# Hybrid decoder layer on one core: the query projection reads the residual times the norm weight, and the root of its norm is applied to the attention scores

## The chip, the cores and the metric

One core of a Trainium2 chip (trn2) runs the whole program as one launch. TensorE (PE), VectorE (DVE), ScalarE (ACT), GpSimd (POOL) and SyncE (SP) work in parallel and wait for one another by semaphores; SyncE issues nearly all DMA. TensorE's clock has two levels, 1.2 and 2.4 GHz, and the profile shows which one was granted. The metric is the device time of a launch in microseconds, the median of several runs.

## The reference

One step of a decoder layer for 264 tokens of width 2048: one prompt of 256 and 8 sample sequences of one token. All data is fp32. Cut to the part around the change:

```python
mix = concat(s5_out, m2_out) @ w_out            # 2048 x 2048
x = x + mix
xn = rmsnorm(x, norm_xa_w)                      # x / sqrt(mean(x^2) + eps) * w
q = (xn @ xa_wq)                                # 4 heads of 512
s = einsum('blhd,bmhd->bhlm', q, k) * 512 ** -0.5
att = softmax(s)                                # over 256 memory tokens
x = x + einsum('bhlm,bmhd->blhd', att, v) @ xa_wo
x = x + hier_moe(rmsnorm(x, norm_ffn_w))        # 32 experts
```

The prompt's keys and values are computed in the kernel from 256 memory tokens; those of the 8 samples are caches in HBM (keys and values of 8 x 256 x 4 x 512).

## The kernel before

Activations are held transposed: 16 blocks of 128 features (partitions) by 264 tokens, XT for the residual, xn for the input of a projection. A projection with a 2048 x 2048 weight takes 8 slabs of 2 MB (256 output columns each), streamed by SyncE through a ring of four slots. TensorE makes one output block of 128 features out of 16 fp32 matmuls (128x128 weights, 264 columns; the trace counts two passes for each). A slab is two blocks, and its slot is reloaded once its second block is done.

The work is cut into stages, each an `nc.Block`; all engines meet at its end before any begins the next. The stages around the change:

1. **Gate and norms** (lines 1503 to 1545). VectorE's `norm_dve` (367) writes the normed Mamba half into `xn[:, 8:16]` and, last in the stage, the normed S5 half into `xn[:, 0:8]`. Their sources u and z are blocks of `h`, which lies in `H`, a part of the buffer SH.
2. **`project_add_norm("w_out", ...)`** (1554). SyncE first issues two "side slabs" of sample keys (`put_side`, 230) into SH, then w_out's slabs in a loop (`load_matrix_loop`) and, with `load_through`, the first query slabs as slots come free. `project_pe` (292) runs the 16 blocks in a loop on TensorE. Per block VectorE adds the result into XT (1598), ScalarE squares it (355) and GpSimd adds the square into block 0 of sqA (1587). Behind block 15: TensorE sums over partitions by a matmul with ones (1578), ScalarE takes the root (357), VectorE the reciprocal (370), and 16 `scalar_tensor_tensor` (372) write xn = XT * weight * 1/root. The same function, with the experts' norm and the router's weights, runs behind attention for xa_wo.
3. **Attention** (1642 to 2018). TensorE runs the 16 query blocks (1801, unrolled, four per head) in two PSUM banks, ScalarE copies each into Q (1945). In the blocks of head h + 1 TensorE also does the small work of head h: GpSimd widens the sample queries (1685), TensorE turns them into rows (1698), spreads each over the partitions (1710), and VectorE multiplies them by the sample keys in a side slab (1887); prompt scores (1718), row maxima (1866, 1867), exponentials on ScalarE with `scale=SCALE` (1962), transposes of the weights (1728), outputs (1741). Head 3 has no further query block over it. The sample values come through the ring, except those of head 2, which take the two side slabs once head 3's keys are used up (`side_used`, 1892, then 1662 to 1666); `sample_outputs` (1761) waits for them. SyncE's queue then goes on with xa_wo's slabs.

What sets the order in the attention stage is the program order of each engine, written out by hand, with semaphore counts; SyncE's program order (1651 to 1667) mixes query slabs, keys and values.

## Time and profile before

| | |
|---|---|
| Runs | 1696.13 us median of 3 (1691.56 to 1696.76) |
| The profiled execution | 1695.85 us, span of its instructions 1694.1 us |
| Mean granted TensorE clock | 0.958 of full |
| Busy: TensorE matmul, weight load | 1554.9 us (92%), 1095.4 us (65%) |
| Busy: VectorE, ScalarE, GpSimd | 743.7, 323.3, 213.9 us |
| DMA | 376.17 MB, mean 222 GB/s |

How to read it: times are from the start of the span. A row of a timeline gives the start, the duration, the engine, the line of the kernel, the operation with what it writes and reads, how many of them run together, and in brackets how long the engine had been idle and what released it. PEld is TensorE's weight load, which overlaps its matmuls. Ends of matmuls are modelled.

### The profile page before, as it was taken

The numbers are of one execution on the slowest core, as the hardware profiler recorded it, in microseconds if no ns is written. First come the engines' busy times: TensorE is split into PE (matmuls) and PEld (weight loads), VectorE is DVE, ScalarE is ACT, GpSimd is POOL, SyncE is SP. The second block draws the span as 40 slices with busy tenths as digits, with TensorE's granted clock in tenths as the row PEclk, the third lists the DMA queues.
The fourth block names the chain that finished last, engine by engine and source line by source line (L and its number), as shares of the span: only waits on it lengthen the run. The fifth ranks groups of instructions, "written<-read, shape, count | busy, mean of one in ns | idle before, by whom it ended". The sixth has DMA issues, their size and how long they took to land. (4 is left out here: it accounts for less than half of the span.)

```text
span 1694.1 us, 20979 instructions
## 1 busy us (share of the span) xinstructions
PE 1554.9 (92%) x8111; PEld 1095.4 (65%) x8111; DVE 743.7 (44%) x2004; ACT 323.3 (19%) x857; POOL 213.9 (13%) x305
## 2 busy tenths in 40 slices
PE   7999998989889788997999699958999999999996
PEld 5888876767677676886888378735445445445444
DVE  3537429999974642002334300061333333333344
ACT  3111101111022321000111100032212212212214
POOL 1111026565620000110000001120000000000000
PEclk9999998999999899998999899968999999999999
DMA  9743443333341556442576866404999999999981
GB/s 275 229 150 113 137 150 112 112 112 112 112 139 67 172 173 218 146 146 92 176 257 232 300 197 233 160 39 168 400 403 403 383 403 401 385 405 402 382 335 51
DMA packets 203311, 376.17 MB, mean 222 GB/s; under 512 B 24931, under 2 KB 158351, under 8 KB 178370
## 3 DMA queue, kind: packets, MB, share of 16 engines
q1 hardware_dynamic: 198554, 370.62, 60.1%
q10 hardware_dynamic: 4664, 4.28, 0.7%
q8 instruction: 62, 1.02, 0.2%
q14 instruction: 31, 0.25, 0.0%
HBM read 363.44 MB, written 11.54 MB: 221 GB/s over the span
## 5 line engine op out<-in xcount | busy, mean ns | idle before, releaser
L923 PE MATMUL ps<-ring,M 128*128 128x256 f32 x1024 | 247.7, 400 | 1.6 <-ACT M L936 1.6
L306 PE MATMUL ps<-X,ring 128*128 128x264 f32 x1024 | 232.0, 390 | 7.5 <-PEq L1503 6.4
L923 PEld LDWEIGHTS ps<-ring,M 128*128 128x128 f32 x1024 | 201.9, 201 | 43.0 <-issue 14.5
L306 PEld LDWEIGHTS ps<-X,ring 128*128 128x128 f32 x1024 | 197.0, 193 | 42.4 <-issue 8.1
L2393 PE MATMUL ps<-ring,M 128*64 128x512 f32 x1024 | 223.3, 594 | 0.3 <-ACT M L2482 0.3
L636 PE MATMUL ps<-X,ring 128*128 128x264 f32 x896 | 204.6, 389 | 0.0
L636 PEld LDWEIGHTS ps<-X,ring 128*128 128x128 f32 x896 | 170.4, 192 | 29.3 <-issue 0.4
L2393 PEld LDWEIGHTS ps<-ring,M 128*64 128x64 f32 x1024 | 72.2, 137 | 137.7 <-issue 137.0
L1801 PE MATMUL ps<-X,ring 128*128 128x264 f32 x512 | 120.2, 392 | 9.4 <-PEq L1555 9.4
L1801 PEld LDWEIGHTS ps<-X,ring 128*128 128x128 f32 x512 | 98.4, 194 | 27.3 <-issue 9.8
L2437 PE MATMUL ps<-SH,M 128*64 128x512 f32 x512 | 113.4, 595 | 1.4 <-DVE XT L2610 1.4
L1598 DVE TENSOR_TENSOR XT<-XT,ps 128x264 f32 x32 | 13.7, 430 | 220.9 <-PE ps L306 220.9
L2599 DVE TENSOR_TENSOR work<-ps,SH 128x512 f32<-128x512 f32 x64 | 44.3, 692 | 142.4 <-ACT SH L2512 142.4
L2405 PE MATMUL ps<-SH 128*128 128x264 bf16 x512 | 90.3, 280 | 3.8 <-DVE work L2604 3.8
L2610 DVE TENSOR_TENSOR XT<-XT,ps 128x264 f32<-128x264 f32 x256 | 88.8, 426 | 1.7 <-PE ps L2405 1.7
L2592 DVE SCALAR_TENSOR_TENSOR M<-M,work,ps 128x256 f32<-128x256 f32 x16 | 7.7, 481 | 171.4 <-ACT M L2489 171.4
L2437 PEld LDWEIGHTS ps<-SH,M 128*64 128x64 f32 x512 | 36.2, 137 | 67.5 <-issue 67.5
L1587 POOL TENSOR_TENSOR M<-M 128x264 f32<-128x264 f32 x30 | 22.2, 741 | 445.3 <-ACT M L355 445.3
L2376 PE MATMUL ps<-SH,M 128*128 128x224 bf16 x512 | 72.2, 265 | 6.1 <-issue 6.1
L2405 PE MATMUL ps<-SH,work 128*128 128x264 bf16 x256 | 71.5, 279 | 0.0
L355 ACT ACTIVATE M<-XT 128x264 f32<-128x264 f32 x48 | 18.6, 418 | 237.4 <-DVE XT L1598 228.2
L2405 PEld LDWEIGHTS ps<-SH 128*128 128x128 bf16 x512 | 34.6, 98 | 40.8 <-issue 12.2
(444 smaller groups left out, 1789.7 us busy)
## 6 DMA issues: line engine op xcount, KB each, us to landing
SH<-in_moe_w_down SPq DMA_DIRECT2D x32, 2048.0 KB, 12.6
ring<-in_moe_w_gate SPq DMA_DIRECT2D x64, 1024.0 KB, 11.9
ring<-in_moe_w_up SPq DMA_DIRECT2D x64, 1024.0 KB, 14.2
ring<-in_w_in SPq DMA_DIRECT2D x14, 2048.0 KB, 8.8
ring<-in_xa_wk SPq DMA_DIRECT2D x8, 2048.0 KB, 9.2
ring<-in_xa_wv SPq DMA_DIRECT2D x8, 2048.0 KB, 9.1
ring<-in_w_out SPq DMA_DIRECT2D x8, 2048.0 KB, 8.8
SH<-in_cache_mem_k SPq DMA_DIRECT2D x8, 2048.0 KB, 9.8
```

Of the source, the lines that this page charges most:

```text
L306: mm = nc.tensor.matmul(ps[:, b, 0:T], w[:, k, o * P:(o + 1) * P], xn[:, k, :], start=(k == 0), stop=(k == KB - 1))
L355: nc.scalar.activation(sq[:, k, 0:n], src[:, k, 0:n], ACT.Square).then_inc(squares.sem, squares.up())
L636: mm = nc.tensor.matmul(ps[:, n % 4, 0:T], w[:, d, o * P:(o + 1) * P], xn[:, d, :], start=(d == 0), stop=(d == KB - 1))
L923: mm = nc.tensor.matmul(ps[:, kv_bank(s), a * 256:(a + 1) * 256], memT[:, k, a * P:(a + 1) * P], w[:, k, :], start=(k == 0), stop=(k == KB ...
L1587: nc.gpsimd.tensor_tensor(sqA[:, 0, :], sqA[:, 0, :], sqA[:, k, :], ALU.add).then_inc(squares_added.sem, squares_added.up())
L1801: mm = nc.tensor.matmul(ps[:, k % 2, 0:T], w[:, d, o * P:(o + 1) * P], xn[:, d, :], start=(d == 0), stop=(d == KB - 1))
L2376: mm = nc.tensor.matmul(ps[:, 6 + f % 2, (k % 2) * 4 * CAP:(k % 2 + 1) * 4 * CAP], x_parts[part][:, a, k * P:(k + 1) * P], picked[:, q % 2 ...
L2393: mm = nc.tensor.matmul(ps[64 * e:64 * e + 64, 0, :], xg[:, p % 3, k, e, :], gate_up_unit(e, half)[:, :, k % 8, :], start=(k == 0), stop=( ...
L2405: mm = nc.tensor.matmul(ps[:, 2 + d % 4, 0:T], out_parts[i][:, d * P:(d + 1) * P], slot_of[:, p % 2, :], start=(i == 0), stop=(i == 2))
L2437: mm = nc.tensor.matmul(ps[64 * e:64 * e + 64, 2 + n, :], g_midT[:, f * P + 64 * e:f * P + 64 * e + 64], down_unit(e)[:, f, 512 * n:512 * ...
L2599: v.tensor_tensor(out_rest[:, c], ps[:, 2 + n, :], out_parts[0][:, c], ALU.subtract).then_inc(outs_rest.sem, 1)
L2610: v.tensor_tensor(XT[:, d, :], XT[:, d, :], ps[:, 2 + d % 4, 0:T], ALU.add).then_inc(scatter_taken.sem, 1)
```

## The change

- The w_out projection becomes a stage of its own. It reads its input from `h`, so the gate stage writes the normed halves there (z in place, S5 into u) and xn is free.
- Per block of it ScalarE now writes xn = XT * weight, without the root, and then the square; for block 15 the copy alone. GpSimd adds the squares of blocks 0 to 14. The ones matmul, root, reciprocal and 16 scalings are not in this stage.
- In the attention stage ScalarE first squares block 15 (into the buffer `rstd`). Behind query block 0 TensorE does six small matmuls (`sums`): sums of squares of the prompt tokens as two columns (tokens on partitions), and of the 8 samples as 8 columns equal in all partitions. ScalarE takes the root of these 10 columns, VectorE the reciprocal and, for the prompt, the product with 512 ** -0.5.
- The prompt's scale goes into the row maxima and the exponentials; that of the samples into GpSimd's widening, now a multiplication.
- Q moves to the start of H, where `h` is no longer needed. So the second half of the second side slab moves behind it, and that slab is loaded by two DMAs of 1 MB instead of one of 2 MB, each time.

```diff
@@ -227,11 +227,20 @@
+SIDE_LOADS = (16, 32)
+def side_part(i, j, n=1):
+    at = 4096 * i + 512 * j if 8 * i + j < 12 else 6144 + 4224 + 512 * (j - 4)
+    return SH[:, at:at + 512 * n]
...
     i = u % 2
-    sp.dma_start(unit(4 + i).rearrange("p (j d) -> p j d", d=DX), of_samples(name, u)).then_inc(
-        side_loaded[i].sem, side_loaded[i].up(16))
+    n = 8 // (i + 1)
+    for j in range(0, 8, n):
+        sp.dma_start(side_part(i, j, n).rearrange("p (j d) -> p j d", d=DX),
+                     of_samples(name, u)[:, j:j + n, :]).then_inc(side_loaded[i].sem, side_loaded[i].up(16))
@@ -289,7 +298,7 @@
-def project_pe(pe, name, first_slab=0, count=None):
+def project_pe(pe, name, source, first_slab=0, count=None):
@@ -303,7 +312,7 @@
             for k in range(KB):
-                mm = nc.tensor.matmul(ps[:, b, 0:T], w[:, k, o * P:(o + 1) * P], xn[:, k, :],
+                mm = nc.tensor.matmul(ps[:, b, 0:T], w[:, k, o * P:(o + 1) * P], source[:, k, :],
@@ -1537,11 +1546,11 @@
     def _(dve):
-        norm_dve(dve, z, xn[:, 8:16, :], m2_wc, 8, T, 1)
+        norm_dve(dve, z, z, m2_wc, 8, T, 1)
...
             nc.vector.tensor_tensor(xn[:, o, :], sig[:, o, :], u[:, o, :], ALU.mult).then_inc(gated.sem, gated.up())
-        norm_dve(dve, xn, xn, s5_wc, 8, T, 2)
+        norm_dve(dve, xn, u, s5_wc, 8, T, 2)
@@ -1550,15 +1559,52 @@
     "router_coarse_weights_loaded", "router_fine_weights_loaded", "squares_added"))
+last_square = rstd[:, 0:T]
+weighted = signal("weighted_block_ready")
+with nc.Block() as block:
+    @block.sync
+    def _(sp):
+        for u in range(2):
+            put_side(sp, "cache_mem_k", u)
+        load_matrix_loop(sp, "w_out", 40)
+        load_through(sp, 44)
+    @block.tensor
+    def _(pe):
+        project_pe(pe, "w_out", h)
+    @block.scalar
+    def _(act):
+        for k in range(KB):
+            act.wait_ge(block_taken.sem, block_taken.at(k + 9))
+            nc.scalar.activation(xn[:, k, :], XT[:, k, :], ACT.Copy, scale=w_xa[:, k:k + 1]).then_inc(
+                weighted.sem, weighted.up())
+            if k < KB - 1:
+                nc.scalar.activation(sqA[:, k, :], XT[:, k, :], ACT.Square).then_inc(squares.sem, squares.up())
+    @block.gpsimd
+    def _(pool):
+        for k in range(1, KB - 1):
+            pool.wait_ge(squares.sem, squares.at(k + 1))
+            if k > 1:
+                pool.wait_ge(squares_added.sem, squares_added.at(k - 1))
+            nc.gpsimd.tensor_tensor(sqA[:, 0, :], sqA[:, 0, :], sqA[:, k, :], ALU.add).then_inc(
+                squares_added.sem, squares_added.up())
+    @block.vector
+    def _(dve):
+        def take(k, b):
+            x = XT[:, bass.ds(k, 1), :]
+            return nc.vector.tensor_tensor(x, x, ps[:, b:b + 1, 0:T], ALU.add)
+        project_take(dve, "w_out", take)
+Signal.stage()
...
             first, n = G[name]
-            if name == "w_out":
-                for u in range(2):
-                    put_side(sp, "cache_mem_k", u)
@@ -1573,7 +1619,7 @@
         def _(pe):
-            project_pe(pe, name)
+            project_pe(pe, name, xn)
@@ -1601,16 +1647,14 @@
-project_add_norm("w_out", w_xa, 44)
-Q = H[:, 2048:2048 + KB * T].rearrange("p (k t) -> p k t", t=T)
+Q = H[:, 0:KB * T].rearrange("p (k t) -> p k t", t=T)
...
 nmax, rsum = (st8[:, 16 * i:16 * i + 8].rearrange("p (h a) -> p h a", a=2) for i in range(2))
+q_root, q_scale, row_scale = st8[:, 32:42], st8[:, 48:58], st8[:, 64:66]
@@ -1631,6 +1675,7 @@
      "sample_weights_zeroed", "sample_queries_widened"))
+q_sums, q_rooted, q_scaled = (signal(f"att_{n}") for n in ("square_sums_done", "roots_ready", "scales_ready"))
@@ -1682,8 +1727,11 @@
                 pool.wait_ge(qt_done.sem, qt_done.at(h))
-            gp.tensor_copy(q_wide, Q[:, 4 * h:4 * h + 4, TP:T].unsqueeze(2).to_broadcast([P, 4, 16, TS])).then_inc(
-                wide_copied.sem, wide_copied.up())
+            else:
+                pool.wait_ge(q_scaled.sem, q_scaled.at(1))
+            gp.tensor_tensor(q_wide, Q[:, 4 * h:4 * h + 4, TP:T].unsqueeze(2).to_broadcast([P, 4, 16, TS]),
+                             q_scale[:, 2:10].unsqueeze(1).unsqueeze(1).to_broadcast([P, 4, 16, TS]),
+                             ALU.mult).then_inc(wide_copied.sem, wide_copied.up())
@@ -1765,15 +1813,15 @@
                     pe.wait_ge(side_loaded[half].sem, side_loaded[half].n)
-                    v = by_sample(unit(4 + half))
+                    value = lambda j, a: side_part(half, 2 * j + a)
...
                     pe.wait_ge(*loaded(g))
-                    v = by_sample(slot(g))
+                    value = lambda j, a: by_sample(slot(g))[:, j, a, :]
...
                         mm = nc.tensor.matmul(ps[32 * j:32 * j + 32, SPV, :], sPT[:, h, a, 4 * half + j, :],
-                                              v[:, j, a, :], start=(half == 0 and a == 0),
+                                              value(j, a), start=(half == 0 and a == 0),
@@ -1787,6 +1835,18 @@
             mm.then_inc(ft_done.sem, ft_done.up())
+        def sums():
+            pe.wait_ge(squares.sem, squares.at(1))
+            parts = (sqA[:, 0, :], last_square)
+            for a in range(2):
+                for i, x in enumerate(parts):
+                    nc.tensor.matmul(ps[:, 7, a:a + 1], x[:, a * P:(a + 1) * P], ones[:, 0:1],
+                                     start=(i == 0), stop=(i == 1))
+            for i, x in enumerate(parts):
+                mm = nc.tensor.matmul(ps[:, 7, 2:10], ones[:, :], x[:, TP:T], start=(i == 0), stop=(i == 1))
+            mm.then_inc(q_sums.sem, q_sums.up())
@@ -1802,6 +1862,8 @@
                     mm.then_inc((q_done if o == 0 else slab_used).sem, (q_done if o == 0 else slab_used).up())
+                if k == 0 and d == KB - 1:
+                    sums()
@@ -1864,7 +1926,7 @@
             st(v.tensor_reduce(nmax[:, h, :], ps[:, SCORE, :].rearrange("p (a m) -> p a m", a=2), AX.X, ALU.max))
-            v.tensor_scalar(nmax[:, h, :], nmax[:, h, :], -SCALE, None, ALU.mult).then_inc(
+            v.scalar_tensor_tensor(nmax[:, h, :], nmax[:, h, :], -1.0, row_scale, ALU.mult, ALU.mult).then_inc(
@@ -1878,13 +1940,12 @@
                 i = b // 4
-                dve.wait_ge(side_loaded[i].sem, side_loaded[i].at(16 * h))
+                dve.wait_ge(side_loaded[i].sem, side_loaded[i].at(SIDE_LOADS[i] * h))
             dve.wait_ge(qrow_done.sem, qrow_done.at(n + 1))
-            keys = by_sample(unit(4 + b // 4))
...
                     dve.wait_ge(sscore.sem, sscore.at(2 * n + a))
-                v.tensor_tensor_reduce(junk8, keys[:, b % 4, a, :], ps[:, 3 + n % 2, :], 1.0, 0.0,
+                v.tensor_tensor_reduce(junk8, side_part(b // 4, 2 * (b % 4) + a), ps[:, 3 + n % 2, :], 1.0, 0.0,
@@ -1917,6 +1978,10 @@
+        dve.wait_ge(q_rooted.sem, q_rooted.at(1))
+        st(v.reciprocal(q_scale, q_root))
+        v.tensor_scalar(row_scale, q_scale[:, 0:2], SCALE, None, ALU.mult).then_inc(q_scaled.sem, q_scaled.up())
+        dve.wait_ge(q_scaled.sem, q_scaled.at(1))
@@ -1960,7 +2025,7 @@
                 nc.scalar.activation(Pm[:, h % 2, a, :], ps[:, SCORE, a * MEM:(a + 1) * MEM], ACT.Exp,
-                                     bias=nmax[:, h, a:a + 1], scale=SCALE,
+                                     bias=nmax[:, h, a:a + 1], scale=row_scale[:, a:a + 1],
@@ -1990,10 +2055,15 @@
+        nc.scalar.activation(last_square, XT[:, KB - 1, :], ACT.Square).then_inc(squares.sem, squares.up())
...
             take_query(4 * q)
+            if q == 0:
+                act.wait_ge(q_sums.sem, q_sums.at(1))
+                nc.scalar.activation(q_root, ps[:, 7, 0:10], ACT.Sqrt, scale=1.0 / D,
+                                     bias=eps_c[:, 0:1]).then_inc(q_rooted.sem, q_rooted.up())
```

## Rows read from the trace of the kernel before

**Rows 1.** The page: busy time of the engines, and GB/s in 40 equal slices.

```profile
PE 1554.9 (92%) x8111; PEld 1095.4 (65%) x8111; DVE 743.7 (44%) x2004; ACT 323.3 (19%) x857; POOL 213.9 (13%) x305
GB/s 275 229 150 113 137 150 112 112 112 112 112 139 67 172 173 218 146 146 92 176 257 232 300 197 233 160 39 168 400 403 403 383 403 401 385 405 402 382 335 51
```

**Rows 2.** Timeline of the seam between the w_out stage and the attention stage.

```profile
765.75 8.17 PE L306 MATMUL ps<-X,ring 128*128 128x264 f32 x36
766.96 0.43 DVE L1598 TENSOR_TENSOR XT<-XT,ps 128x264 f32 x1 [6.69 <-PE ps L306]
...
774.08 0.43 DVE L1598 TENSOR_TENSOR XT<-XT,ps 128x264 f32 x1 [6.69 <-PE ps L306]
774.54 0.42 ACT L355 ACTIVATE M<-XT 128x264 f32<-128x264 f32 x1 [6.70 <-DVE XT L1598]
...
775.84 0.71 PE L1578 MATMUL ps<-M,ones 128*128 128x264 f32 x2 [1.91 <-POOL M L1587]
...
777.10 1.80 DVE L370 RECIPROCAL rstd<-rstd 128x264 f32<-128x264 f32 x1 [2.59 <-ACT rstd L357]
778.94 6.56 DVE L372 SCALAR_TENSOR_TENSOR X<-XT,par,rstd 128x264 f32<-128x264 f32 x16
...
786.00 11.18 PE L1801 MATMUL ps<-X,ring 128*128 128x264 f32 x37 [9.45 <-PEq L1555]
```

**Rows 3.** Stretches: PE, PEld, DVE, ACT, POOL busy; clock, DMA share, GB/s.

```profile
776.00:778.00 2.00, 0.55 (x2) 0.13 (x2) 0.90 (x1) 0.48 (x1) 0.00 (x0) 0.96 1.05 358
786.00:800.00 14.00, 14.00 (x51) 11.53 (x52) 0.00 (x0) 0.38 (x1) 2.45 (x6) 0.80 0.00 1
```

**Rows 4.** Waits in 780 to 1000: who waited for what, total, times, longest.

```profile
PE ps L1775 <- DMA SH<-in_cache_mem_v: 11.7, 1, 11.7
```

**Rows 5.** Timeline of the seam between the attention stage and the xa_wo stage.

```profile
980.83 0.66 PE L1787 MATMUL ps<-ident,M 128*128 128x128 f32 x4 [0.71 <-ACT M L1991]
981.52 0.26 DVE L1916 COPY X<-ps 128x16 f32<-128x16 f32 x2 [4.68 <-PE ps L1787]
982.59 9.74 PE L306 MATMUL ps<-X,ring 128*128 128x264 f32 x35 [1.10 <-PEq L1642]
```

**Rows 6.** Timeline of attention where head 3's queries are widened.

```profile
924.15 0.61 POOL L1685 COPY SH<-SH 128x512 f32<-128x512 f32 x1 [35.02 <-ACT SH L1945]
925.30 0.91 PE L1698 MATMUL ps<-ident,SH 128*128 128x128 f32 x6 [1.41 <-ACTq L1982]
```

**Rows 7.** Busy time by stretch, around that idle time.

```profile
920.00:930.00 10.00, 8.59 (x45) 7.02 (x43) 2.43 (x6) 2.75 (x6) 0.61 (x1) 1.00 1.05 388
```

**Rows 8.** Busy time by stretch, at the seam before xa_wo.

```profile
980.00:990.00 10.00, 8.19 (x34) 6.54 (x31) 0.26 (x2) 0.59 (x1) 0.00 (x0) 0.83 1.07 348
```

**Rows 9.** Timeline of TensorE at 512, small matmuls among projections.

```profile
512.33 0.29 PE L1223 MATMUL ps<-wtmp,tri 128*128 128x16 f32 x2
...
513.14 1.54 PE L923 MATMUL ps<-ring,M 128*128 128x256 f32 x6
```

**Rows 10.** Timeline of attention where head 0's queries are widened.

```profile
817.91 0.61 POOL L1685 COPY SH<-SH 128x512 f32<-128x512 f32 x1 [28.90 <-ACT SH L1945]
820.82 1.05 PE L1698 MATMUL ps<-ident,SH 128*128 128x128 f32 x8
```

**Rows 11.** GpSimd's groups by line and shape, busy and mean ns.

```profile
L1037 POOL TENSOR_TENSOR X<-X,wtmp 128x256 f32<-128x256 f32 x32 | 30.3, 946 | 2.5
L2130 POOL TENSOR_TENSOR M<-M 128x512 f32<-128x512 f32 x4 | 4.5, 1151 | 12.8 <-ACT M L2166 12.8
```

**Rows 12.** Busy time by stretch, before and in the wait for the last value slab.

```profile
937.00:941.00 4.00, 4.00 (x33) 1.34 (x36) 3.13 (x12) 0.59 (x1) 0.00 (x0) 1.00 0.01 2
943.00:945.00 2.00, 2.00 (x25) 0.66 (x18) 1.70 (x5) 0.00 (x0) 0.00 (x0) 1.00 0.77 256
945.00:967.00 22.00, 8.79 (x60) 5.09 (x52) 4.55 (x18) 2.90 (x6) 0.00 (x0) 0.81 1.05 387
```

**Rows 13.** Busy time by stretch, between attention and the experts.

```profile
1116.00:1150.00 34.00, 19.39 (x107) 12.51 (x106) 16.07 (x51) 11.40 (x23) 10.56 (x14) 0.70 0.01 2
```

## The prediction

> **What bounds the kernel now.** I read from coarse to fine: the page's busy shares, busy time by stretch, the timeline of each seam between stages, the granted clock there, then the waits. The page gives TensorE 92% of the span [rows 1]: what lets TensorE start earlier shortens the kernel unless a later wait takes it back. In the stretch of the change a projection block of 16 matmuls takes 7.12 us, the distance between two of VectorE's additions into XT (766.96 to 774.08), and the blocks follow each other without a gap [rows 2].
>
> The hole is at the seam. The last w_out block is added at 774.08 and its square taken at 774.54; GpSimd adds that, TensorE sums over partitions at 775.84, and behind the root come VectorE's reciprocal at 777.10 (1.80 us) and the 16 scalings of the norm, 6.56 us from 778.94. TensorE starts the query projection at 786.00. Between the end of its last w_out matmul (765.75 + 8.17 = 773.92) and 786.00 it did 0.71 us of work [rows 2]. The hole also costs clock: the granted clock is full (2.4 GHz) up to just before 778, and of the 14 us from 786 to 800 its mean of 0.80 means 5.6 us at half (1.2 GHz) [rows 3].
>
> A second hole lies in the same stage: TensorE waits 11.7 us, once, for a value slab by DMA in the third head's sample outputs [rows 4]. The page's chain of waits is of no use here, since it holds only the last 25 us.
>
> **Part 1, the norm leaves the seam.** Removed between the last addition and the query projection: the last square with its addition, the sum matmul, the root, the reciprocal, 16 scalings. Left: the addition (774.08, 0.43 us) and one ScalarE instruction, the copy times weight of block 15. Its nearest row is the square of the same shape, 0.42 us from 774.54, so it ends at 774.96 [rows 2]. Then the barrier between stages. At the other seam where TensorE comes without long idle time, VectorE's last copies end at 981.52 + 0.26 = 981.78 and TensorE starts at 982.59: 0.81 us [rows 5]. At the present one it is 786.00 - (778.94 + 6.56) = 0.50 us, after a long wait [rows 2]. I take 0.81, because TensorE now also has to leave its loop just then: start at 775.77, **10.2 us earlier**. Ends: 775.46 with 0.50 us; and 776.65 if leaving the loop is what ends last, since TensorE's first instruction behind the loop stands at 775.84 and 0.81 follows. So 9.4 to 10.5 us. SyncE's issue of the last query slab waits for the same matmul as VectorE's addition and is shorter than what follows that: it doesn't hold the barrier.
>
> **Part 2, the clock.** The gap becomes 773.92 to 775.77, 1.85 us, with full work on both sides. A TensorE idle time of 1.41 us inside the query stage (before 925.30, [rows 6]) left the clock at 1.00 for the whole stretch 920 to 930 [rows 7]. I take it that it holds: 5.6 us at half speed were 2.8 us lost, and **2.8 us** come back. Against it speaks the seam at 980 to 983: idle times of 0.71 and 1.10 us with four transposes between them [rows 5], and a clock of 0.83 over 980 to 990, so 3.4 us at half and 1.7 us lost [rows 8]. The Trainium skill ("TensorE: Matmul & The Clock Gate", its parts on the clock gate and on transposes) says that idleness throttles the array and that transposes do not count as busy in the same way. By that the seam at 980 was emptier than its busy time says, and a poor model of a gap between plain matmuls; this trace cannot separate the two.
>
> **Part 3, what is put in.** (a) Six fp32 matmuls of 1 or 8 columns behind query block 0, on TensorE's path. Nearest: four fp32 matmuls of 16 columns with 128x128 weights between projections, 512.33 to 513.14 (the first of the four and what follows them), 0.20 us each [rows 9]; six make **1.2 us**. Fewer columns might make them cheaper, so the low end is half, 0.6; the high end is the form with 128 columns, 1.05 us for four [rows 10], 1.6 us for six. Their wait for the last square (ScalarE, at the start of the stage) is over long before block 0 ends. (b) The root of 10 columns on ScalarE, reciprocal and scale on VectorE: covered by query block 1 (7.12 us), since VectorE has nothing before the first head's rows, ScalarE's next job is taking block 1, and GpSimd's first widening comes after block 3. Without that cover, at most the 1.80 us of the 264-column reciprocal and a ScalarE instruction of 0.42. (c) Per block of w_out a second ScalarE instruction, 0.42 us in a period of 7.12 us: nothing. (d) Scales given as columns in the exponentials and the row maxima change no counts: nothing. (e) GpSimd's widening of the sample queries becomes a multiplication of two inputs on 128x512. Now it takes 0.61 us; a two-input operation of that size took 1.15 us (L2130) [rows 11]. Before heads 0 to 2 there is room: it starts at 817.91 and TensorE uses it at 820.82, 2.9 us [rows 10]. For head 3 TensorE comes at once: 924.15 + 1.15 = 925.30, just when TensorE now starts, since it is also held by ScalarE's exponential [rows 6]; with the weight load in front I take **0.1 us**. Ends: 0; and 0.8 us at GpSimd's dearest rate, 946 ns for 256 elements (L1037) [rows 11], which makes 1.89 us for 512.
>
> The Trainium skill ("ScalarE: Activation LUTs", what a table load costs) charges 2.66 us for a switch of function set. The root moves from one stage to the next; should that bring one more switch, uncovered, the sum would be smaller by that figure.
>
> **Part 4, the side slabs.** One more issue at the start of the w_out stage, whose first slabs are loaded by then, and four later on SyncE; key slabs are fetched a head ahead. The last value slab is the exposed one. It lies behind three other slabs in the queue: together 8.4 MB, of which 0.5 move from 943 to 945 at 256 GB/s and the other 7.9 need 20.4 us at 387 GB/s, to 965.4; TensorE goes on at 967, since the next weights mix in [rows 12]. Two halves move the same bytes in the same place: **0**. Ends: 1.9 us gained if the mixing goes; half a slab more of other traffic in front of the second half, 1.0 MB at 387 GB/s, 2.7 us lost.
>
> **Does the gain pass on?** The 11.7 us wait ends with a burst of value slabs, and the burst starts when VectorE has scored half of head 3: from 937 to 941 DMA moved 2 GB/s [rows 12]. So it moves with the stage and the wait keeps its length. Behind attention DMA is idle from 1116 to 1150 (2 GB/s) [rows 13], so the expert stage, in which the queues run full at 380 to 405 GB/s [rows 1], starts when compute lets it.
>
> **Sum.** 10.2 + 2.8 - 1.2 - 0.1 = 11.7 us. The profiled execution took 1695.85 us (span 1694.1), so 1684.15; the median of the runs, 1696.13, lies 0.3 above it: **1684.4 us**, 0.7% less.
>
> **Rivals.**
> - *The clock falls all the same* (15%), as at 982: 1.7 us lost again, 1684.4 + 1.7 = 1686.1 us. For it: the look of that seam. Against: 1.41 us of idle time without a fall. The skill's rule on transposes makes it the less likely.
> - *A DMA wait takes the gain back* (10%). If the burst of value slabs does not move with the stage, the 11.7 us wait grows by the whole gain: 1696 us. For it: it is TensorE's largest wait for DMA in this stretch. Against: the idle queue just before.
> - *GpSimd's multiplication is slow in this form* (5%), the one on the slower side. Its scale is read with a step of zero in two dimensions, which no GpSimd row shows. A duration p costs 3(p - 2.9) + (p - 1.1) us over the four heads. That cancels the 11.8 us of the rest at p = 5.4 us and makes the kernel 5 us slower at p = 6.7 us: 1701 us. Against: no row with 256 columns is above 0.95 us.
> - *The forecast's mechanism*: 70%.
>
> **From these to the numbers.** 0.3%, about 5 us, is what a measurement of this kernel can tell from no change. Forecast and first rival are faster by more than that: 0.85. The second is the same: 0.10. The third is slower: 0.05. Within the forecast the best ends give 10.5 + 2.8 - 0.6 + 1.9 = 14.6 us (1681.5), the worst 9.4 + 2.8 - 1.6 - 0.8 - 2.7 = 7.1 us (1689.0). With a microsecond on either side for the median's own scatter: 1680.5 to 1690.0, which takes in the first rival and leaves out the other two, 15%.
>
> **What the profile of the changed kernel would show.** Right: TensorE idle less than 2.5 us between w_out and the query projection, the clock at 1.00 there, 16 scalings and a 1.80 us reciprocal gone from VectorE, query block 1 later by 1.2 us, GpSimd's widening at about 1.15 us. Wrong: half clock in the first query block; a wait for the last value slab well off 11.7 us; idle time at the query transposes of heads 0 to 2; a table load more on ScalarE's path.

## The result and the profile after

The changed kernel takes **1678.92 us** (median of 4 runs, 1676.59 to 1680.68), the kernel before on the same chip 1693.85 us (4 runs, 1691.08 to 1696.76): ratio 0.9905 [0.9884, 0.9926], 14.9 us less. The forecast was 1684.4 us, 11.7 us less, range 1680.5 to 1690.0: the time lies below the range. What the forecast worked out at the seam came nearly to the number; the rest of the gain came from places to which it gave nothing.

The page of the changed kernel, busy time by engine, against [rows 1]:

```profile
span 1678.9 us, 21005 instructions
PE 1550.0 (92%) x8121; PEld 1093.6 (65%) x8121; DVE 735.7 (44%) x1989; ACT 330.2 (20%) x873; POOL 215.4 (13%) x304
```

TensorE is busy for 4.9 us less though it has 10 more instructions: some matmuls ran at full clock that ran at half before. The span is 15.2 us shorter. So most of the gain, 10.3 us, is idle time. The timeline of the seam between w_out and attention, against [rows 2]:

```profile
774.60 0.43 DVE L1599 TENSOR_TENSOR XT<-XT,ps 128x264 f32 x1 [6.69 <-PE ps L315]
775.06 0.51 ACT L1581 ACTIVATE X<-XT,par 128x264 f32<-128x264 f32 x1 [6.29 <-DVE XT L1599]
...
775.86 0.42 ACT L2058 ACTIVATE rstd<-XT 128x264 f32<-128x264 f32 x1 [0.28 <-PEq L1565]
...
776.03 7.36 PE L1861 MATMUL ps<-X,ring 128*128 128x264 f32 x32 [1.59 <-PEq L1565]
...
783.22 0.28 PE L1845 MATMUL ps<-ones,M 128*128 128x1 f32 x2
...
783.42 0.38 ACT L2010 COPY SH<-ps 128x264 f32<-128x264 f32 x1 [7.14 <-PE ps L1861]
...
784.48 15.82 PE L1861 MATMUL ps<-X,ring 128*128 128x264 f32 x70
...
784.66 0.27 ACT L2065 ACTIVATE M<-ps,eps_c 128x10 f32<-128x10 f32 x1 [0.86 <-PE ps L1848]
...
784.96 0.22 DVE L1982 RECIPROCAL M<-M 128x10 f32<-128x10 f32 x1 [9.94 <-ACT M L2065]
...
791.88 0.38 ACT L2010 COPY SH<-ps 128x264 f32<-128x264 f32 x1 [6.95 <-PE ps L1861]
```

From the last addition to TensorE's first query matmul it takes 776.03 - 774.60 = 1.43 us; it was 11.92 us. The sums, the root and the reciprocal lie behind block 0, and no wait arises from them. Stretches of the changed kernel (columns as in rows 3), against [rows 3]:

```profile
774.00:776.00 2.00, 0.44 (x2) 0.03 (x2) 0.43 (x1) 0.66 (x2) 0.16 (x1) 1.00 0.24 54
...
786.00:800.00 14.00, 14.00 (x65) 11.97 (x64) 0.00 (x0) 0.76 (x2) 0.00 (x0) 1.00 0.47 151
```

The clock stays at 1.00 across a stretch of 2 us in which TensorE is busy for 0.44, and then there are 65 matmuls in 14 us where 51 were.

**Where the 15.2 us come from.** I read the distance between pairs of events that both kernels have (us, the profiled execution of each). "Query block taken" is ScalarE's copy of that block; an addition is VectorE's into XT:

```
stretch                                           before  after   diff  forecast
last w_out addition - query block 1 taken          22.02   8.82 -13.20  -13.0
query block 1 - block 2 taken (the sums)            7.12   8.46  +1.34   +1.2
block 2 - block 16 taken                          120.49 120.49   0.00    0
block 16 taken - first late value slab issued      18.04  17.80  -0.24   +0.1
that issue - TensorE on behind the last slab       25.57  25.48  -0.09    0
there - first xa_wo addition ("xa_wo seam")        24.49  21.94  -2.55    0
xa_wo additions 1 to 16                           106.80 106.80   0.00    0
16th addition - second expert down-projection
  slab issued ("norm and router")                  88.74  87.00  -1.74    0
there - first store of y                          499.07 499.13  +0.06    0
sum                                               912.34 895.92 -16.42  -11.7
```

Ahead of this stretch and behind it the changed kernel lost 0.5 and 0.7 us; that was not followed up. The part ahead differs between traces by more than that: the last w_out addition stands at 771.4 to 776.1 us in the 17 traces of this document, so the distances compare kernels better than whole spans do. Every row that the forecast worked out is right to 0.4 us. The surplus sits in two rows, far behind the change, to which it gave nothing: 4.3 us.

Timeline and stretches of the changed kernel around these two places; against [rows 5, 8] for the first:

```profile
968.43 0.66 PE L1835 MATMUL ps<-ident,M 128*128 128x128 f32 x4 [0.70 <-ACT M L2056]
...
970.04 9.16 PE L315 MATMUL ps<-X,ring 128*128 128x264 f32 x40 [0.96 <-PEq L1687]
...
977.59 0.43 DVE L1644 TENSOR_TENSOR XT<-XT,ps 128x264 f32 x1 [8.21 <-PE ps L315]
```

```profile
943.00:961.00 18.00, 8.40 (x40) 2.60 (x33) 0.10 (x2) 0.58 (x1) 0.00 (x0) 0.64 1.07 371
967.00:977.00 10.00, 8.34 (x43) 6.41 (x36) 0.26 (x2) 0.58 (x1) 0.00 (x0) 1.00 1.06 333
1084.00:1104.00 20.00, 8.82 (x41) 5.86 (x40) 14.14 (x35) 6.58 (x11) 1.51 (x4) 0.74 0.27 105
1111.00:1137.00 26.00, 12.96 (x70) 9.38 (x71) 12.91 (x43) 7.57 (x17) 8.21 (x12) 0.54 0.01 3
```

The same four of the kernel before, as far as they do not stand ahead, 13 to 17 us later:

```profile
991.81 0.43 DVE L1598 TENSOR_TENSOR XT<-XT,ps 128x264 f32 x1 [10.04 <-PE ps L306]
```

```profile
956.00:974.00 18.00, 6.68 (x27) 3.26 (x28) 0.00 (x0) 0.94 (x2) 0.00 (x0) 0.62 1.07 368
1098.00:1118.00 20.00, 8.82 (x36) 5.57 (x35) 14.15 (x35) 6.58 (x11) 1.51 (x4) 0.66 0.28 105
1128.00:1154.00 26.00, 14.56 (x81) 10.77 (x82) 11.32 (x41) 6.27 (x15) 6.54 (x11) 0.54 0.01 2
```

At the xa_wo seam the instructions are the same and the gaps nearly so, 0.70 and 0.96 us beside 0.71 and 1.10; but the clock does not fall. The granted clock read microsecond by microsecond gives the stretches at half clock (TensorE's busy time in them in brackets). Before: 777-792, which is 13.7 us (5.5); 958-973, 13.7 (5.0); 982-986, 3.4 (3.4); 1102-1116, 13.7 (5.5); 1129-1154, 23.9 (13.9). After: none at the first seam; 942-946, 3.4, and 949-960, 10.2 (3.6 behind the wait); none at the xa_wo seam; 1089-1100, 10.2 (3.1); 1112-1137, 23.9 (12.7). Half of the busy time at half clock is lost. At the xa_wo seam that is (3.4 + 5.0 - 3.6) / 2 = 2.4 us of the 2.55; in norm and router (5.5 + 13.9 - 3.1 - 12.7) / 2 = 1.8 of 1.74. So both extra gains are clock: the same work lost less to half clock. Why the clock steps elsewhere in the same work is what the experiments are about.

### The profile page after: what moved, and what is told of

It reads as the page before. It is cut to its first block and busy times, and to the rows that moved or that the text cites. A ratio compares the mean times of both kernels' runs of the same rounds, so it can differ in the third digit from the quotient of the medians.

```text
span 1678.9 us, 21005 instructions
## 1 busy us (share of the span) xinstructions
PE 1550.0 (92%) x8121; PEld 1093.6 (65%) x8121; DVE 735.7 (44%) x1989; ACT 330.2 (20%) x873; POOL 215.4 (13%) x304
## 5 line engine op out<-in xcount | busy, mean ns | idle before, releaser
L645 PE MATMUL ps<-X,ring 128*128 128x264 f32 x896 | 205.1, 390 | 0.0
L645 PEld LDWEIGHTS ps<-X,ring 128*128 128x128 f32 x896 | 171.0, 192 | 29.2 <-issue 0.4
L315 PE MATMUL ps<-SH,ring 128*128 128x264 f32 x512 | 116.1, 391 | 6.4 <-PEq L1512 6.4
L1861 PE MATMUL ps<-X,ring 128*128 128x264 f32 x512 | 117.7, 387 | 1.6 <-PEq L1565 1.6
L315 PE MATMUL ps<-X,ring 128*128 128x264 f32 x512 | 114.2, 387 | 1.0 <-PEq L1687 1.0
L315 PEld LDWEIGHTS ps<-SH,ring 128*128 128x128 f32 x512 | 98.7, 193 | 23.8 <-issue 6.8
L315 PEld LDWEIGHTS ps<-X,ring 128*128 128x128 f32 x512 | 97.3, 190 | 17.6 <-issue 1.2
L1861 PEld LDWEIGHTS ps<-X,ring 128*128 128x128 f32 x512 | 96.6, 190 | 18.5 <-issue 2.0
L1599 DVE TENSOR_TENSOR XT<-XT,ps 128x264 f32 x16 | 6.9, 429 | 110.5 <-PE ps L315 110.5
## 6 DMA issues: line engine op xcount, KB each, us to landing
ring<-in_moe_w_up SPq DMA_DIRECT2D x64, 1024.0 KB, 13.8
```

Of the source, the lines that this page charges most:

```text
L315: mm = nc.tensor.matmul(ps[:, b, 0:T], w[:, k, o * P:(o + 1) * P], source[:, k, :], start=(k == 0), stop=(k == KB - 1))
L645: mm = nc.tensor.matmul(ps[:, n % 4, 0:T], w[:, d, o * P:(o + 1) * P], xn[:, d, :], start=(d == 0), stop=(d == KB - 1))
L1599: return nc.vector.tensor_tensor(x, x, ps[:, b:b + 1, 0:T], ALU.add)
L1861: mm = nc.tensor.matmul(ps[:, k % 2, 0:T], w[:, d, o * P:(o + 1) * P], xn[:, d, :], start=(d == 0), stop=(d == KB - 1))
```

## The experiments

The theories, in the words of this text. *Moments*: the clock steps at moments of its own, so that where a stretch of work comes in time decides how much of it is at half clock; a delay of a microsecond or two upstream can switch several microseconds on or off downstream. *Work*: the change gained them by what it does (less DMA or VectorE work near the waits, a shorter hole). *Scatter*: they differ between executions anyway. In the quoted expectations theory A is scatter; theory B is, in the first runs, "the change moved them for good", and from sums_two on the moments.

The two kernels unchanged. The experiments ran on four chips, each beside runs of the kernel before on the same chip, to which its ratio refers. The changed kernel ran again on two of them: beside warm_hole and hole_back (after_again), and beside warm_waits_again and sums_two_warm (after_third). For the other experiments a difference to it crosses chips; the kernel before had medians of 1693.7 to 1694.6 us on the four.

> The kernel before, unchanged, for a second profile. Theory A (the 4.0 us that the changed kernel gained behind the query stage, beyond the 11.3 of the seam itself, are the clock, by chance of the execution): the stretches at half clock fall elsewhere than in the first profile; the stretch at 982 to 986, right at the start of the xa_wo projection, is absent or of another length, and the first xa_wo block (9.22 us from its first matmul to VectorE's addition) may take 7.6 us. Theory B (the change moved them for good): the half clock at 982 to 986 comes again, first xa_wo block 9.2 us. Both: the seam before the query projection 11.9 us, first query block between 9.5 and 10.5 us.

> The changed kernel, unchanged, timed in five rounds, with a second profile. Theory A: the mean gain over many runs is nearer 12 than 16 us, ratio about 0.992 to 0.993, and the stretches at half clock behind attention differ from the first profile. Theory B: 15 to 16 us, ratio 0.990 to 0.991, and they stand where they stood: none at the start of the xa_wo projection, first xa_wo block 7.6 us. Both: last addition of w_out to first query matmul 1.4 us, first query block 7.4 us.

> The changed kernel once more, beside its warmed form on the same chip: ratio to the kernel before 0.990 to 0.991, and the trace's half-clock stretches as in its first two profiles (3.4 us and 10.2 us around the value wait, none at the xa_wo seam).

Before: 1695.19 us in one run, and a median of 1694.62 (1688.77 to 1698.25) over 23 others on that chip. After: 1679.46 us (5 runs, 1677.03 to 1681.5), ratio 0.9907 [0.9887, 0.9927], and 1679.68 (6 runs), 0.9911 [0.9891, 0.9931]. The distances are those of the first profiles to 0.2 us in every row; all are in this table:

```
                  seam q1-q2 q16-v1 v1-PE xa_wo  norm,  to y    sum
                                           seam router store
before            22.02 7.12 18.04 25.57 24.49 88.74 499.07 912.34
before_again      22.05 7.12 18.04 25.66 24.32 88.81 499.07 912.36
split_only        21.88 7.12 18.03 25.50 24.32 88.92 499.11 912.17
before_sums       21.97 8.46 18.04 25.41 22.06 87.13 499.13 909.49
warm_hole         19.28 7.12 18.03 24.28 24.75 89.33 499.05 909.13
hole_back         19.53 8.46 17.81 25.09 21.83 87.08 499.00 906.09
after              8.82 8.46 17.80 25.48 21.94 87.00 499.13 895.92
after_again        8.83 8.46 17.80 25.62 21.92 87.06 499.06 896.04
after_third        8.84 8.46 17.80 25.64 21.94 87.05 499.09 896.10
hole_short        12.37 8.46 17.80 25.58 21.72 86.97 499.00 899.18
sums_two           8.83 9.80 17.81 25.49 24.60 88.97 499.04 901.83
sums_three         8.83 12.83 17.80 25.70 24.56 89.04 499.02 905.07
pool_twice         8.87 8.46 20.55 25.30 22.37 87.35 499.11 899.30
warm_waits         8.83 8.46 17.81 25.66 21.90 86.33 499.13 895.41
warm_waits_again   8.84 8.45 17.81 25.73 21.90 86.20 499.06 895.28
sums_two_warm      8.86 9.80 17.81 25.57 20.22 84.58 501.08 895.20
warm_all           8.83 8.46 17.81 25.53 20.76 90.95 499.10 898.72
```

(Blocks 2 to 16 and the 16 additions, 120.49 and 106.8 us in all of them, are left out of the table and stand in the sum. v1 is the first late value slab.) The places repeat in the two traces of the kernel before and the three of the changed one, on different chips, so scatter falls for these stretches. Each experiment below has one trace. The time as a whole does scatter: over the 23 runs of the kernel before it goes with the mean granted clock of the run (correlation -0.82, 1.6 us per 0.001). Where in the kernel the untraced runs differ, no run shows.

**The second slab in two halves, alone** (on the kernel before).

```diff
-    sp.dma_start(unit(4 + i)..., of_samples(name, u))
+    n = 8 // (i + 1)
+    for j in range(0, 8, n):
+        sp.dma_start(unit(4 + i)...[:, j:j + n, :], of_samples(name, u)[:, j:j + n, :])
```

> The kernel before with one thing of the change: every second side slab (four of the keys, the last of the values) is loaded by two DMAs of 1 MB in place of one of 2 MB, into the same bytes. Forecast's view: 0 us, TensorE goes on behind the last value slab at the same distance from the issue of the value slab before it (25.6 us) within 0.5 us. Rival: the split shortens or lengthens that wait by 2 us, and carries part of what the seam does not explain; ratio 0.998 or less.

(VectorE's wait for these keys counts both halves.) 1696.16 us against 1694.39, ratio 1.0006 [0.9988, 1.0024]. Its largest wait for the slab, against the 11.7 of [rows 4]:

```profile
PE ps L1777 <- DMA SH<-in_cache_mem_v: 11.6, 1, 11.6
```

The split costs and gains nothing, and the two extra gains are not its doing.

**The hole kept, with its clock held up** (on the kernel before). 18 more matmuls of `ones` by a square, unused, behind the sum matmul.

```diff
+    if name == "w_out":
+        for _ in range(18):
+            nc.tensor.matmul(ps[:, 0, 0:T], ones[:, :], sqA[:, 1, :], start=True, stop=True)
```

> The kernel before, with 18 matmuls of ones by a block of squares (8.0 us of TensorE work into a free PSUM bank, result unused) behind the sum matmul of w_out's norm. The norm stays in the seam, only the clock is kept up. Forecast's view: TensorE's first query matmul as before, 11.9 us after the last addition; clock 1.00 through the seam; first query block 7.4 us in place of 10.1, so 2.7 us faster, ratio 0.9984. Rival (the clock is no part of the gain, or the extra matmuls delay VectorE or the barrier): no change in time, or first query block still above 9 us.

1691.15 us (12 runs), 0.9979 [0.9966, 0.9992]. Timeline and stretch of this kernel:

```profile
775.28 8.17 PE L1582 MATMUL ps<-M,ones 128*128 128x264 f32 x36
...
784.86 8.47 PE L1804 MATMUL ps<-X,ring 128*128 128x264 f32 x37 [1.41 <-PEq L1555]
```

```profile
776.00:786.00 10.00, 8.60 (x39) 7.07 (x38) 8.35 (x17) 0.00 (x0) 1.33 (x1) 1.00 0.46 153
```

With the idle time filled the seam takes 19.28 us instead of 22.02: 2.7 us, the "2.8 us" of part 2 measured by itself.

**The hole put back, long and short** (on the changed kernel). 20 or 4 squares of XT into `rstd`, unused, at the end of ScalarE's w_out stage.

```diff
+        for _ in range(20):   # hole_short: range(4)
+            st(nc.scalar.activation(rstd[:, 0:T], XT[:, 0, :], ACT.Square))
```

> The changed kernel with 20 squares of 264 columns one after the other on ScalarE (result unused) behind the last copy of the w_out stage: the hole is back without the norm's work, some 9 to 10 us long. If the gain is the seam and the clock there, 9.5 + 2.7 us come back: 12 us slower than the changed kernel, 1.5 to 3 us faster than the kernel before, ratio to before 0.998 to 0.999. If something else in the change (Q in another place, the split slab, the multiplication) carries part of the 15 us, this kernel stays 4 us or more faster than the kernel before, ratio 0.9975 or less.

> The changed kernel with four squares of 264 columns one after the other on ScalarE behind the last copy of w_out, which lengthens the gap of TensorE at the seam from 1.9 to about 3.9 us. If a gap of that length leaves the clock alone: 2 us slower than the changed kernel, clock 1.00, first query block 7.4 us. If the clock falls there: up to 2 us more, first query block 8 to 9.5 us, ratio to the kernel before 0.993.

hole_back: 1693.22 us, 0.9989 [0.9976, 1.0001]: nearly the whole gain is gone, 13.8 us by the medians. (Its profiled execution took 1689.19 us, 4 us below its median; there the stretch of the table is 10.0 us longer than in after_again, 906.09 against 896.04. What the other 3.8 us of the median are is not seen.) hole_short: 1684.51 us, 0.9944 [0.9926, 0.9962]; its profiled execution 1681.76. Timelines of hole_back and of hole_short, and a stretch of hole_short:

```profile
773.91 9.04 ACT L1587 ACTIVATE rstd<-XT 128x264 f32<-128x264 f32 x20
...
783.58 8.94 PE L1864 MATMUL ps<-X,ring 128*128 128x264 f32 x32 [10.71 <-PEq L1565]
```

```profile
772.86 1.77 ACT L1587 ACTIVATE rstd<-XT 128x264 f32<-128x264 f32 x4
...
775.26 9.05 PE L1864 MATMUL ps<-X,ring 128*128 128x264 f32 x32 [3.44 <-PEq L1565]
```

```profile
776.00:780.00 4.00, 4.00 (x13) 3.12 (x13) 0.00 (x0) 0.00 (x0) 1.75 (x6) 0.65 0.87 283
```

1.85 us more of idle time (3.44 instead of 1.59) make the clock fall and the seam 3.5 us longer: the idle time itself and 1.7 us for 3.4 us at half. So at this place the changed seam kept its clock with less than 2 us to spare. The xa_wo seam stayed at 21.8 and 21.7 us in both traces although the hole was back: the shorter hole did not gain it.

**The sums twice and three times** (on the changed kernel): the six small matmuls issued again, same results.

```diff
+        for _ in range(2):   # sums_three: range(3)
             ... the six matmuls of sums()
```

> The changed kernel with the six small matmuls of sums() done twice. By the forecast the block costs 1.2 us (the first trace says 1.3), so query block 1 is taken 1.3 us later and so is everything to the wait for the value slab. If what the changed kernel gains behind attention hangs on where its work stands against the moments at which the clock steps (theory B), the later parts need not be 1.3 us later: the shift at the first xa_wo addition against the changed kernel lies anywhere from 0 to 3 us, in steps of about 1.7 us beside the 1.3, and the stretches of half clock differ. If the later gain comes from the code itself, it is 1.3 us everywhere.

> The changed kernel with the six small matmuls done three times: 2.7 us more on TensorE's path. With them twice, 1.3 us more cost 6 us. If the loss is that of the clock behind attention and does not grow with the delay (theory B), three times costs about as much as twice or less, 3 to 7 us against the changed kernel, ratio to the kernel before 0.992 to 0.995, and the trace shows 2.7 us up to the value wait and the rest at the xa_wo seam and in the router. If each repetition costs 6 us by itself, 12 us and ratio 0.998.

sums_two: 1685.6 us (8 runs), 0.9952 [0.9933, 0.997], where the changed kernel has 0.9907 and 0.9911: some 6 us more by the medians, and **5.8 us more in the stretch of the table (901.83 against 896.04), for an added 1.34 us**. The rest is at the two places, 24.60 against 21.92 and 88.97 against 87.06, which are the values of the kernel before. Timeline (a line of it) and stretches of sums_two:

```profile
978.42 0.43 DVE L1644 TENSOR_TENSOR XT<-XT,ps 128x264 f32 x1 [9.98 <-PE ps L315]
```

```profile
943.00:961.00 18.00, 7.18 (x29) 3.65 (x30) 0.00 (x0) 1.17 (x2) 0.00 (x0) 0.62 1.08 367
967.00:977.00 10.00, 8.46 (x32) 6.83 (x33) 0.26 (x2) 0.44 (x1) 0.00 (x0) 0.83 1.08 350
1086.00:1106.00 20.00, 9.75 (x38) 6.19 (x39) 13.72 (x34) 6.27 (x11) 1.52 (x4) 0.66 0.28 105
```

0.83 in 967 to 977 is the 0.83 of [rows 8], and 0.66 the 0.66 of the kernel before. sums_three: 1685.68 us, 0.9952 [0.9934, 0.997]; both places long again, and the stretch 9.0 us longer than in the changed kernel. The sums themselves cost 12.83 - 8.46 = 4.37 us and not 2.7, because the clock fell just behind them:

```profile
784.00:789.00 5.00, 5.00 (x16) 3.99 (x17) 0.39 (x2) 0.27 (x1) 0.00 (x0) 0.66 0.00 0
```

That is 3.4 us at half, 1.7 us lost. TensorE had no idle time there that the trace shows; from 5.0 to 1.1 us ahead of the fall stand 3.9 us of matmuls of 1 and 8 columns. With 2.7 us of them, in sums_two, the clock held. The median is only 6.0 us above after_third's, and the profiled execution's whole span, 1684.9 us, is only 6.0 to 7.0 us above the changed kernel's three: its last w_out addition stands at 771.39 us, 2.1 to 3.2 us earlier than in the three traces of the changed kernel. In sums_two and sums_two_warm it stands at 771.40 and 771.46; why, ahead of all that was edited, was not followed up.

**The delay alone, in the kernel before**: the six matmuls on squares that nobody reads, behind query block 0.

```diff
+        if first block:
+            six matmuls of sqA[:, 0, :], sqA[:, 1, :] and ones into ps[:, 7, ...]
```

> The kernel before with six small matmuls of the same shapes (results unused) behind query block 0: nothing but a delay of 1.3 us on TensorE. Theory B: the kernel before stands where the half-clock stretches behind attention are long already (13.7 us in the value wait, 3.4 at the xa_wo seam), so this delay costs its own 1.3 us or less, down to a gain of 3 us if it moves the tail to the good place; ratio 0.998 to 1.001. Rival (a delay at this point always costs 6 us): ratio 1.0035.

1691.9 us (12 runs), 0.9988 [0.9975, 1.0001]: work added, time not longer, and the stretch 2.9 us shorter (909.49 against 912.34). Timeline (a line of it) and stretches of before_sums:

```profile
990.57 0.43 DVE L1598 TENSOR_TENSOR XT<-XT,ps 128x264 f32 x1 [8.20 <-PE ps L306]
```

```profile
979.00:989.00 10.00, 8.34 (x48) 5.81 (x40) 0.26 (x2) 0.58 (x1) 0.00 (x0) 1.00 0.93 296
1098.00:1118.00 20.00, 9.61 (x43) 6.41 (x44) 13.72 (x34) 6.41 (x11) 1.51 (x4) 0.74 0.28 105
```

1.34 us of delay put both places at the values of the changed kernel, in a kernel with nothing else of the change. The interval reaches 1.0001, so of the time alone only "not slower" is sure; the places are the proof. Together with sums_two this speaks for the moments and against the work: the same work is short or long by when it comes.

The steps themselves say it too. The last w_out addition stands at 774.08 us in the kernel before and at 774.14 in before_sums, and from query block 2 to the value wait the work of the second is 1.35 us later. Microseconds in which the clock steps, in the kernel before, then in before_sums:

```profile
972.00:973.00 1.00, 1.00 (x5) 0.85 (x4) 0.00 (x0) 0.00 (x0) 0.00 (x0) 0.80 1.10 349
1102.00:1103.00 1.00, 0.00 (x0) 0.00 (x0) 1.00 (x1) 0.00 (x0) 0.00 (x0) 0.55 1.04 434
```

```profile
972.00:973.00 1.00, 1.00 (x8) 0.84 (x5) 0.00 (x0) 0.58 (x1) 0.00 (x0) 0.81 1.11 350
1102.00:1103.00 1.00, 0.00 (x0) 0.00 (x0) 0.96 (x3) 0.00 (x0) 0.00 (x0) 0.55 0.97 410
```

The clock rises within 972 and falls within 1102 in both, to a few hundredths of a microsecond, though the work in them is not the same. And the fall near the value wait comes at 958.7 in the kernel before, but before_sums has one at 955.3 already, 3.4 us earlier for work that is 1.35 us later. The steps do not travel with the work.

**GpSimd's multiplication twice** (on the changed kernel), ahead of each head's widening.

```diff
+            st(gp.tensor_tensor(q_wide, ..., ALU.mult))
```

> The changed kernel with GpSimd's multiplication done twice ahead of each head. Each is 1.18 us in the first trace; so 1.2 us later per head. Room before heads 0 to 2 (2.9 us): nothing there. Head 3: query transposes 1.2 us later than in the changed kernel, 2.7 us after the last query block is taken where it was 1.7. Rival: the small work of heads 0 to 2 is late too, and query block 16 is taken over 1 us later. In the whole: 1.2 us, and by theory B up to 6 us, as with the sums done twice.

1682.96 us (4 runs), 0.9935 [0.9909, 0.996], 3.3 above after_third's median on another chip; the stretch is 3.2 us longer. Heads 0 to 2 did not notice (120.49 us unchanged); head 3 did. Timeline of the changed kernel, then timeline and stretch of pool_twice:

```profile
912.37 0.38 ACT L2010 COPY SH<-ps 128x264 f32<-128x264 f32 x1 [6.54 <-PE ps L1861]
...
912.83 1.18 POOL L1732 TENSOR_TENSOR SH<-SH,M 128x512 f32<-128x512 f32 x1 [34.45 <-ACT SH L2010]
...
914.06 1.16 PE L1746 MATMUL ps<-ident,SH 128*128 128x128 f32 x8 [1.51 <-POOL SH L1732]
```

```profile
911.17 1.18 POOL L1732 TENSOR_TENSOR SH<-SH,M 128x512 f32<-128x512 f32 x1 [33.08 <-ACT SH L2013]
...
912.43 1.28 POOL L1735 TENSOR_TENSOR SH<-SH,M 128x512 f32<-128x512 f32 x1
...
913.77 2.07 PE L1749 MATMUL ps<-ident,SH 128*128 128x128 f32 x8 [2.87 <-POOL SH L1735]
```

```profile
911.00:919.00 8.00, 5.23 (x22) 4.77 (x23) 2.36 (x6) 2.20 (x6) 2.46 (x2) 0.79 1.05 387
```

The multiplication takes 1.18 us, and one more costs 2.75 us at head 3: 1.3 of its own, the rest because the clock fell behind 2.87 us of idle time, for 3.4 us.

**The clock held up in the later waits** (on the changed kernel): unused matmuls ahead of the wait for the last value slab and in the router's norm; then with the sums twice; then in the router as well.

```diff
+    if router:
+        for _ in range(18): matmul(ps[:, 0, 0:T], ones, sqA[:, 1, :])
+    if h == 2 and half == 1:
+        for _ in range(20): matmul(ps[:, 3, 0:MEM], ones, V[:, 0, 0:MEM])
```

sums_two_warm adds `for _ in range(2):` around sums(). warm_all adds to the first version 9, 1 and 1 matmuls of ones by XT (264 columns) ahead of the router's three waits for its rows, 12 behind the transposes of its gates, and 1 and 2 of ones by V around attention's last transposes.

> The changed kernel with work of no use that holds the clock up in two later waits: 20 matmuls of ones by V (128x256) ahead of the wait for the last value slab, and 18 matmuls of ones by squares (128x264) behind the sum matmul of the norm after xa_wo; free PSUM banks, results unused. If the clock behind waits costs what the rows say (3.5 us of busy time at half behind the value wait, 3.0 us and more behind the norm), the kernel gains 1.7 + 1.5 us and perhaps 1 to 2 more in the router, ratio to the kernel before 0.988 to 0.989. Rival: the extra matmuls hold TensorE beyond the end of the wait or the clock falls later all the same: no gain, ratio 0.9905.

> The changed kernel with idle matmuls in two waits (20 of 128x256 ahead of the last value slab's, 18 of 128x264 in the norm after xa_wo), a second time with more runs. Theory: 1 to 3 us faster than the changed kernel, ratio to the kernel before 0.988 to 0.990. Rival: no different from the changed kernel.

> The small matmuls done twice (1.3 us of delay) in the kernel with two warmed waits. Theory B: what made that delay cost 6 us was the half clock in the value wait and behind the norm; with the clock held up there it costs 1.3 us, at most 3 with the xa_wo seam, against the warmed kernel. Rival: the 6 us have another cause, and come here too.

> The kernel with two warmed waits (value slab, norm after xa_wo), and idle matmuls at further places: 1 and 2 at the xa_wo seam, 9 and 1 and 1 between the router's transposes of sample rows, 12 behind its last transposes. The half-clock stretches left in the trace of the warmed kernel (3.4 us at the xa_wo seam, 23.9 us with 13.6 busy in router and first gather) should shrink: up to 1.7 + 6.8 us gained on the changed kernel beyond the 2 us of the first two places; I expect 5 to 8 us in all, ratio to the kernel before 0.986 to 0.988. Rival: half of the router's busy time is waits for other engines, and the clock buys nothing: ratio 0.9895.

warm_waits 1677.02 us (0.9894 [0.986, 0.9928]) and again 1680.12 (0.9913 [0.9894, 0.9932]); sums_two_warm 1677.51 (0.9904 [0.9885, 0.9924]); warm_all 1681.64 (0.9926 [0.9906, 0.9946]). None can be told from the changed kernel by its time, so neither the 1 to 3 us and more expected of the filled waits nor the 5 to 8 us expected of warm_all came. Stretches of warm_waits_again, then of sums_two_warm:

```profile
943.00:957.00 14.00, 12.97 (x64) 8.81 (x68) 0.26 (x2) 0.00 (x0) 0.00 (x0) 0.88 1.06 380
967.00:977.00 10.00, 8.34 (x34) 6.52 (x31) 0.26 (x2) 0.58 (x1) 0.00 (x0) 0.83 1.07 347
```

```profile
940.00:960.00 20.00, 17.10 (x94) 11.92 (x94) 0.47 (x4) 1.58 (x3) 0.00 (x0) 1.00 1.07 371
1080.00:1100.00 20.00, 16.83 (x83) 12.02 (x82) 14.14 (x35) 6.51 (x11) 1.52 (x4) 1.00 0.28 106
```

The pair agrees: doubling the sums costs 5.8 us in the stretch where the clock is left alone, and -0.1 us (895.20 against 895.28) with the filling. (The medians on their common chip differ by -2.6 us, 1677.51 against 1680.12; in the traces 4.0 us of difference lie ahead of the last w_out addition, so that number is not one of the sums.) It is not that the filled kernels are free of half clock: the xa_wo seam, 24.60 us in sums_two, takes 20.22 here and 21.90 in warm_waits_again, where the clock still steps down for 3.4 us although TensorE was busy for 12.97 of the 14 us from 943 to 957, and sums_two_warm has 2.0 us more in the experts, 501.08 for 499.06. In warm_all the timeline shows the filling itself in the way:

```profile
1123.62 7.64 PE L2199 MATMUL ps<-XT,ones 128*128 128x264 f32 x24
...
1135.97 0.93 PE L2459 MATMUL ps<-SH,M 128*128 128x224 bf16 x4 [4.71 <-issue]
```

Its 12 matmuls (two passes each) took 7.64 us, the first 4.1 of them at half clock, and held the end of the stage, so that the gather behind them came later: norm and router 90.95 us instead of 87.06.

## Why the prediction was right and wrong

**Part 1, 10.2 us, and part 2, 2.8 us: right.** 13.20 us measured for 13.0. TensorE started 1.43 us behind the last addition; forecast 775.77 - 774.08 = 1.69. Copy times weight takes 0.51 us, not 0.42. Of "I take it that it holds" hole_short shows the margin: at 3.44 us of idle time it no longer holds. On the root: it starts at 784.66, ScalarE having been idle for 0.86 us, with no table load ahead of it, and both profiles have 16 loads of 1.28 us each, so the 2.66 us of the Trainium skill ("ScalarE: Activation LUTs", table loads) did not come into play.

**Part 3, 1.2 + 0.1 us: right.** The sums cost 1.34 us, within 0.6 to 1.6; columns made no difference to their pace, 0.2 us each with 1, 8 or 16 (but see sums_three). The widening: 1.18 us for 1.15, transposes 1.69 us behind the last query block instead of 1.59. That the late slabs' issue still came 0.24 us sooner was not followed up.

**Part 4, 0 us: right** (split_only, 1.0006). The wait itself reads 9.6 us where the text said "keeps its length", 11.7:

```profile
955.65 3.64 PE L1823 MATMUL ps<-SH,work 128*32 128x512 f32 x16 [9.60 <-DMA SH<-in_cache_mem_v]
```

But from issue to going on it is 25.48 us for 25.57: the work ahead of the wait ran partly at half clock and used some of it up. For a wait that ends with a transfer the distance from the issue is the number to compare.

**"Does the gain pass on?": this step failed.** It asked only of DMA queues, and took the stretches behind for fixed. They hold four stretches of half clock, 54.7 us together before (13.7 + 3.4 + 13.7 + 23.9), partly in waits and small work [rows 8, 12, 13]. The change moved the work by 13.2 - 1.3 us against the clock's steps, and less of it fell into half clock: 4.3 us of the 4.7 by which this stretch beat the forecast. That this is a matter of when the work comes, before_sums and sums_two show; that it came out as a gain is luck, for 1.34 us more delay would have taken all of it away. The rows for it were on the table: [rows 8] cost 1.7 us in a seam with gaps of only 0.71 and 1.10 us, while 1.41 us in [rows 6] cost nothing. The text took that for evidence on one seam (the first rival, clock falls at the new seam, which didn't come); it was evidence that a fall depends on more than the gap, and so on more than what the change edits. The range, built from the ends of the change's own terms, had no term for it. The Trainium skill's remark that transposes do not count as busy in the same way ("TensorE: Matmul & The Clock Gate", PE-mode transpose) doesn't explain it alone: with the same four transposes that seam fell in before and sums_two, and not in after and before_sums.

The time lies 5.5 us below the forecast. Of these 3.2 are gain (14.9 us for 11.7), and the other 2.3 are the base: 1696.13 us from three runs, 1693.85 and 1694.62 when measured with more. On the old base the measured gain gives 1681.2 us, just inside the range, so it took both to leave it. The account of the gain: forecast gain 11.7, places 4.3, other stretches 0.4, outside the stretch -1.2, profile against median -0.3, together 14.9.

**The rivals.** The clock's fall at the new seam did not come. The wait for the value slab did not take the gain back. GpSimd's form was not slow (1.18 us), and pool_twice shows that a longer one is felt at one head in four, with 2.75 us for 1.28.

**What stays open.** The traces show the clock's steps at the same place of the work in each of the two or three traced executions of a kernel, and elsewhere in the work after 1.34 us of delay; what fixes those moments, and so which delay is a good one, I have not worked out. That the untraced runs have them at the same places is taken from the medians, not seen. The 4.7 us by which the traces differ ahead of the change, the 3.8 us of hole_back's median and the -0.24 us are open too.

## What to carry to other kernels

Where stretches at half clock lie behind the edit, put a term for them into the range: here 4 to 5 us in 1690, a quarter of this change's gain and as large as many a smaller change, and of either sign. Before a small gain or loss is put down to an edit, compare distances between events stretch by stretch, and try the same edit with a delay of a microsecond and with the clock held up. A projection that needs no normed input, with the norm's factor applied to the small result, takes a whole chain of engines out of a seam; here that was 13.2 us for 1.3.

## What the hardware showed that I had not expected

- 1.34 us of extra TensorE work costs 5.8 us of the stretch in one kernel (sums_two) and gives 2.9 us back in another that does nearly the same (before_sums; by the time, 0.9988 [0.9975, 1.0001], not slower).
- The clock stepped at the same moments, 972.4 and 1102.1 us, in two kernels whose work stood differently there (before, before_sums).
- Behind 3.9 us of matmuls of 1 and 8 columns, without idle time, the clock fell (sums_three); behind 2.7 us of them it did not (sums_two).
- An idle time of 1.59 us kept the clock at the changed seam; 2.87 us (pool_twice, at head 3) and 3.44 us (hole_short) did not; 0.70 to 1.10 us at the xa_wo seam sometimes did not either.
- A factor given as a column makes ScalarE slower at these sizes: copy 0.51 us beside a square's 0.42, exponential 0.56 us beside 0.47 with a constant. Off the path here.
- fp32 matmuls of 1, 8 and 16 columns all follow each other at about 0.2 us.
